# The fourth swish gate tile of each retention head is made among the projections, and the head's work is put in a new order

## The chip, the cores and the metric

The kernel runs on one core of one Trainium2 chip, as one launch. The metric is device time in microseconds (us). TensorE multiplies (PE; its weight load is shown apart as PEld), VectorE (DVE) and ScalarE (ACT) do the arithmetic around it, GpSimd (POOL) does a part of the subtractions and sums, and SyncE (SP) issues most of the loads. All engines run their own instruction stream and meet at semaphores.

## The reference

One layer of a streaming encoder on 640 frames (512 of a new stream, 8 streams of 16 frames): a feed-forward half step, a mixer, a second feed-forward half step, with layer norms between. All matrices are float32. The mixer is what matters here:

```
cb, cc, ch, q, k, v, g, gc, gr = jnp.split(x @ w_in, offsets, axis=-1)
yc, new_buf = short_conv(cc * ch, conv_buf, conv_w)
y_conv = (cb * yc) @ w_conv_br
o, S_new = retention_seq(qh, kh, vh, S0.astype(jnp.float32))      # 4 heads, rotary on q and k
mu = o.mean(-1, keepdims=True)
var = jnp.square(o - mu).mean(-1, keepdims=True)
o = ((o - mu) * lax.rsqrt(var + GN_EPS)).astype(x.dtype).reshape(B, T, D_RET_V)
y_ret = (o * jax.nn.silu(g)) @ w_ret_br
m = jax.nn.sigmoid(gc) * y_conv + jax.nn.sigmoid(gr) * y_ret
return m @ w_out, new_buf, S_new.astype(x.dtype)
```

D_MODEL is 1024, a head has keys of 256 and values of 512, so `g` has 512 columns for each of the 4 heads: four tiles of 128. The states of the 8 running streams (256 x 512 float32 for each head) are read, used and written.

## The kernel before, in words

Each float32 matrix is split into a rounded high part and the low rest, and a product is made as three matmuls (`mm3`, L1034): low by high, high by low, high by high. Activations stand transposed (`xh`, `xl`: 128 partitions x 8 tiles x 640 frames).

Two ways lead to a block of `x @ w`. A unit (L1067) makes one tile of 128 output columns for all 640 frames: 2 halves x 8 tiles of depth x 3 = 48 matmuls of 320 columns. A quad (L1436) makes two such tiles by Winograd's form of Strassen's method: seven products of 4 tiles of depth x 3 = 84 matmuls instead of 96, at the price of sums of weights (POOL, DVE), of their highs (ACT) and lows (DVE), and of sums of the results (DVE). The quads of the mixer are listed in `PROJECTIONS` (L182), 31 of them, in four groups; after each group of four kinds (`cc`, `ch`, `q`, `k`) come swish gates (`s0` to `s5`), merge gates (`gc`, `gr`) and `cb`. `s0` to `s3` hold the first two gate tiles of heads 0 to 3, `s4` and `s5` the third tile of two heads each. A swish quad's result gets its sigmoid from ACT, is multiplied on DVE and is stored to DRAM (`swish_scratch`).

The fourth gate tile of each head was a unit made within the head (`unit_of_chunk`, L1678). Weights for units come in chunks of 512 KB through four slots; PE releases a slot when it is done with the chunk, SP and POOL reload it (raw and high part).

The four heads run one after the other (`head`, L1647). On PE a head is: the values `v` (4 chunks), transposes of rotated keys, scores, `cross(0)` (the queries of half of the running streams by their states; it reads `state`), the outputs of the four prompt tiles (`vh` by `sch`), the gate unit, `cross(1)` (the other half of the streams; all four DMAs of the second state group must have landed), transposes of the normalised outputs (`on`) in four PSUM banks, the first half of the kept state (`knh` by `vh`), the transpose of the sample tile (`on5`), the second half, four state products (`km` by `vp`), and the branch product with `w_ret` (L1624 for its first two units, which wait three times for `head_ready`: for the gated tiles 0 and 1, then 2 and 3, then 4).

On DVE the head takes the statistics of the four prompt tiles, their aggregate, asks ACT for the square root, makes the inverse root with one Newton step and normalises four tiles; it finishes the gate tile; then it does the same chain once more for the sample tile; then five gating products (`ogt`), of each of which ACT makes the high (`ogh`) and DVE the low part (`ogl`), and between them it copies the kept state out of PSUM (`sp`). `psum_free` counts banks that have been read, in order, so a wait for a count is a wait for all reads before it. SP issues the four state loads as soon as `cross(0)` is done (L826), then the load of the gate tiles from `swish_scratch`, then weights.

Of the kernel before, what the change touches and what calls it, by code (L numbers as in the profile page):

```python
# [178 lines left out]
def high_loads_of_slot(c):  # L179
# [3 lines left out]
PROJECTIONS = [(what, j) for j, more in enumerate((("s0", "s1", "gc1"), ("s2", "s3", "gr1"), ("s4", "gc2", "gr2"),  # L183
                                                 ("s5", "gc3")))
# [195 lines left out]
def build_layer(nc, a):  # L380
# [3 lines left out]
    with ctx:  # L384
# [186 lines left out]
        def load_of_part(n):  # L571
# [51 lines left out]
            sem(n) for n in ("swish_sig_made", "swish_made", "swish_in", "k4_made"))  # L623
        conv_ready = sem("conv_ready")
# [61 lines left out]
        U_V, U_K, U_SC, U_O0, U_OP, U_G = 0, 5, 10, 14, 15, 19  # L686
        U_O1, U_T, U_SP, U_T5, U_S1A, U_OUT, U_S1B, U_S0 = 22, 23, 27, 28, 30, 34, 38, 54
# [31 lines left out]
        def _(sync):  # L719
# [102 lines left out]
            def head_loads(i):  # L822
# [7 lines left out]
                sync.dma_start(sg[:, 0:SWISH_TILES, :], a["swish"][i]).then_inc(swish_in, 16)  # L830
# [187 lines left out]
        def _(pe):  # L1018
# [591 lines left out]
            def cross(group, i):  # L1610


                b = bank()
# [7 lines left out]
                last.then_inc(psum_full, 1 + group)  # L1621
                return b
# [24 lines left out]
            def head(i):  # L1647
# [16 lines left out]
                samples = cross(0, i)  # L1664
# [24 lines left out]
                for d in range(2):  # L1689
# [538 lines left out]
        def _(dve):  # L2228
# [689 lines left out]
            def head(i):  # L2918
# [40 lines left out]
                for t in (PT, *range(PT)):  # L2959
                    hi, lo = (knh[:, t, :], knl[:, t, :]) if t < PT else (k4[0][:, :], k4[1][:, :])  # L2960
                    last = split(hi, lo, kd[:, t, :])
                    if t == PT:
                        last.then_inc(k4_made, 1)
                    else:
                        step(last)
# [301 lines left out]
```

## Time and profile before

| | us |
|---|---|
| median of 3 runs | 1758.77 (1758.43 to 1758.84) |
| profiled execution | 1758.78 |
| its span, first to last instruction | 1757.0 |

| engine | busy us | share of the span | instructions |
|---|---|---|---|
| PE | 1746.3 | 99% | 10680 |
| PEld | 1634.4 | 93% | 10680 |
| DVE | 1395.0 | 79% | 1924 |
| ACT | 730.5 | 42% | 1219 |
| POOL | 415.6 | 24% | 296 |

The busy time of a matmul is its time from start to modelled end, and matmuls overlap: in a dense stretch a new one starts every 0.15 us (320 columns) though each is shown as 0.31 us long. So a stretch of matmuls is measured from start to start, not by its mean. Times of DVE and ACT operations can overlap the next one by about 0.1 us in the same way.

### The profile page before, as it was taken

The numbers are of one execution on the slowest core, as the hardware profiler recorded it, in microseconds if no ns is written. First come the engines' busy times: TensorE is split into PE (matmuls) and PEld (weight loads), VectorE is DVE, ScalarE is ACT, GpSimd is POOL, SyncE is SP. The second block draws the span as 40 slices with busy tenths as digits, with TensorE's granted clock in tenths as the row PEclk, the third lists the DMA queues.
The fourth block names the chain that finished last, engine by engine and source line by source line (L and its number), as shares of the span: only waits on it lengthen the run. The fifth ranks groups of instructions, "written<-read, shape, count | busy, mean of one in ns | idle before, by whom it ended". The sixth has DMA issues, their size and how long they took to land.

```text
span 1757.0 us, 27018 instructions
## 1 busy us (share of the span) xinstructions
PE 1746.3 (99%) x10680; PEld 1634.4 (93%) x10680; DVE 1395.0 (79%) x1924; ACT 730.5 (42%) x1219; POOL 415.6 (24%) x296
## 2 busy tenths in 40 slices
PE   9999999999999999999999999999999999999998
PEld 9989999898999999999998989898989989899996
DVE  7888888878898787776267788787868898888986
ACT  5535455443544454544105051414214345454543
POOL 3312112143232223221240212111242212111041
PEclk9999999999999999999999999999999999999999
DMA  8665555434566665733774867676873243333323
GB/s 320 169 185 155 169 156 157 154 98 174 173 184 201 195 193 155 183 95 114 258 241 164 289 216 263 219 257 235 334 288 108 84 129 118 93 105 115 117 93 108
DMA packets 90670, 310.41 MB, mean 177 GB/s; under 512 B 9136, under 2 KB 9520, under 8 KB 90032
## 3 DMA queue, kind: packets, MB, share of 16 engines
q1 hardware_dynamic: 51552, 185.36, 31.2%
q0 software_dynamic: 13696, 50.34, 11.7%
q10 hardware_dynamic: 25296, 72.99, 11.6%
q8 instruction: 85, 1.39, 0.3%
q14 instruction: 41, 0.34, 0.1%
HBM read 267.42 MB, written 75.83 MB: 195 GB/s over the span
## 4 chain that ended last, share of the span: by engine, by line
PE 95%; DVE 3%; issue 1%; ACT 1%; DVEq 0%
PE ps L1024 94%; PE ps L1589 1%; DVE xl L2251 0%; DVE z L2676 0%; DVE z L2779 0%; DVE state L3031 0%; DVE z L2251 0%; PE ps L1498 0%; DVE wql L2251 0%; ACT t L2190 0%; DVE t L2297 0%; ACT xh L1751 0%; DVE y L2814 0%; DVE tl L2251 0%; DVE y L2790 0%
## 5 line engine op out<-in xcount | busy, mean ns | idle before, releaser
L1024 PE MATMUL ps<-th,wql 128*128 128x320 f32 x1136 | 350.9, 309 | 0.0
L1024 PE MATMUL ps<-th,wqh 128*128 128x320 f32 x1136 | 350.7, 309 | 0.0
L1024 PE MATMUL ps<-tl,wqh 128*128 128x320 f32 x1136 | 350.0, 308 | 0.0
L916 POOL TENSOR_TENSOR quad_s<-qraw 128x512 f32<-128x512 f32 x71 | 100.1, 1410 | 709.1 <-DVE wql L2251 322.6
L1024 PE MATMUL ps<-xh,wql 128*128 128x320 f32 x852 | 262.7, 308 | 0.2 <-DVE wql L2251 0.2
L1024 PE MATMUL ps<-xl,wqh 128*128 128x320 f32 x852 | 262.7, 308 | 0.0
L1024 PE MATMUL ps<-xh,wqh 128*128 128x320 f32 x852 | 262.6, 308 | 0.0
L1751 ACT ACTIVATE pu<-ps 128x320 f32<-128x320 f32 x213 | 93.3, 438 | 358.3 <-PE ps L1024 358.3
L2251 DVE TENSOR_TENSOR wql<-quad_s,wqh 128x512 fp32r<-128x512 f32 (+1 forms) x213 | 199.5, 937 | 35.3 <-ACT wqh L1751 34.9
L1024 PEld LDWEIGHTS ps<-tl,wqh 128*128 128x128 f32 x1136 | 213.3, 188 | 0.4
L1024 PEld LDWEIGHTS ps<-th,wql 128*128 128x128 f32 x1136 | 213.2, 188 | 0.4
L1024 PEld LDWEIGHTS ps<-th,wqh 128*128 128x128 f32 x1136 | 213.2, 188 | 0.0
L2251 DVE TENSOR_TENSOR wql<-qraw,wqh 128x512 fp32r<-128x512 f32 x213 | 203.3, 955 | 3.7 <-ACT wqh L1751 3.5
L1751 ACT ACTIVATE wqh<-quad_s 128x512 fp32r<-128x512 f32 (+1 forms) x213 | 163.7, 769 | 53.4 <-PE ps L1024 50.4
L885 POOL TENSOR_TENSOR wl<-raw,wh 128x1024 fp32r<-128x1024 f32 x52 | 131.3, 2526 | 127.4 <-DMA wh<-in_weights 42.2
L1024 PEld LDWEIGHTS ps<-xh,wql 128*128 128x128 f32 x852 | 159.9, 188 | 1.0 <-DVE wql L2251 0.4
L1024 PEld LDWEIGHTS ps<-xl,wqh 128*128 128x128 f32 x852 | 160.0, 188 | 0.4
L1024 PEld LDWEIGHTS ps<-xh,wqh 128*128 128x128 f32 x852 | 160.0, 188 | 0.0
L1751 ACT ACTIVATE wh<-raw 128x1024 fp32r<-128x1024 f32 x67 | 70.3, 1050 | 173.4 <-DMA raw<-in_weights 122.5
L1751 ACT ACTIVATE wqh<-qraw 128x512 fp32r<-128x512 f32 x213 | 132.8, 624 | 10.4 <-PE ps L1024 10.4
L922 POOL TENSOR_TENSOR quad_s<-qraw 128x512 f32<-128x512 f32 x71 | 110.4, 1554 | 67.8 <-DVE wql L2251 67.8
L2251 DVE TENSOR_TENSOR quad_s<-quad_s,qraw 128x512 f32<-128x512 f32 x138 | 105.9, 767 | 23.2 <-POOL quad_s L916 15.6
(293 smaller groups left out, 3764.1 us busy)
## 6 DMA issues: line engine op xcount, KB each, us to landing
qraw<-in_quads SPq DMA_DIRECT2D x142, 512.0 KB, 3.7
raw<-in_weights SPq DMA_DIRECT2D x92, 512.0 KB, 4.6
wh<-in_weights POOLq DMA_DIRECT2D x57, 512.0 KB, 5.2
raw<-sums_scratch SPq DMA_DIRECT2D x32, 512.0 KB, 3.9
state<-in_state_ret ACTq DMA_DIRECT2D x32, 512.0 KB, 7.4
out_ret_sample<-state ACTq DMA_DIRECT2D x32, 512.0 KB, 5.0
sums_scratch<-in_sum_add POOLq DMA_DIRECT2D x8, 1024.0 KB, 9.3
sums_scratch<-sums_scratch POOLq DMA_DIRECT2D x16, 512.0 KB, 6.2
```

Source lines behind the costliest of these rows:

```text
L885: pool.tensor_tensor(w_lo(r), w_raw(r), w_hi(r).bitcast(f32), ALU.subtract).then_inc(chunk_split, 1)
L916: pool.tensor_tensor(qs[:, 0, :], qraw[:, c0, 512:1024], qraw[:, c1, 512:1024], ALU.add).then_inc(pool_sums, 1)
L922: pool.tensor_tensor(qs[:, 2, :], qraw[:, c0, 0:512], qraw[:, c0, 512:1024], ALU.add).then_inc(pool_sums, 1)
L1024: ins = nc.tensor.matmul(out, lhs, rhs, start=start, stop=stop, skip_group_check=adds)
L1589: last = nc.tensor.transpose(cols(k, 128, ps[:, b, :]), src, ident[:, :])
L1751: return nc.scalar.activation(out, in_, ACT.Copy, **kw)
L2251: return V.tensor_tensor(out, x, y, op)
```

## The change

Two quads, `s6` and `s7`, are added to the projections (33 instead of 31); they make the fourth gate tile of two heads each. The gate units, their chunks and what ACT and DVE did for them in the heads are gone. Within a head PE now does `cross(1)` right after the four prompt outputs, then both halves of the kept state, then all transposes, then the state products. DVE takes the sample tile's statistics with the others and runs one chain for five tiles. The copies of the kept state move to ACT.

```diff
-HEAD_CHUNKS = 9
-SWISH_TILES = 3
+HEAD_CHUNKS = 8
-HEAD_BANKS = 62
+HEAD_BANKS = 60
-PROJECTIONS = [... ("s4", "gc2", "gr2"), ("s5", "gc3") ...]
+PROJECTIONS = [... ("s4", "s6", "gc2", "gr2"), ("s5", "s7", "gc3") ...]
-    return [(n, 0), (n, 1)] if n < H else [(2 * (n - H) + m, 2) for m in range(2)]
+    return [(n, 0), (n, 1)] if n < H else [(2 * (n % 2) + m, 2 + (n - H) // 2) for m in range(2)]
...
-                sync.dma_start(sg[:, 0:SWISH_TILES, :], a["swish"][i]).then_inc(swish_in, 16)
+                sync.dma_start(sg[:, :, :], a["swish"][i]).then_inc(swish_in, 16)
...
# PE, head
-                samples = cross(0, i)
+                samples = bank()
+                cross(0, i, samples).then_inc(psum_full, 1)
...
-                assert bk.at - u0 == U_G
-                unit_of_chunk()
-                bk.add()
-                assert bk.at - u0 == U_O1
-                assert cross(1, i) == samples
-                pe.wait_ge(psum_free, u0 + U_G)
-                for dp in range(2):
-                    for t in range(0, PT, 2):
-                        transposed([cols(2 * dp + k, 128, on[:, t + n, :]) for n in range(2) for k in range(2)])
                 assert bk.at - u0 == U_SP
+                assert (u0 + U_O1) % 8 == samples
+                cross(1, i, samples).then_inc(cross_made, 1)
+                pe.wait_ge(keys_split, i + 1)
                 for d in range(2):
...
-                    last.then_inc(psum_full, 1)
-                    if d == 0:
-                        assert bk.at - u0 == U_T5
-                        pe.wait_ge(psum_free, u0 + U_T + 1)
-                        transposed([cols(k, 128, on5[:, :]) for k in range(4)])
+                    last.then_inc(psum_full, 1 + 2 * d)
+                bk.add(2)
+                assert bk.at - u0 == U_T
+                pe.wait_ge(psum_free, u0 + U_SP)
+                for dp in range(2):
+                    for t in range(0, PT, 2):
+                        transposed([cols(2 * dp + k, 128, on[:, t + n, :]) for n in range(2) for k in range(2)])
+                assert bk.at - u0 == U_T5
+                pe.wait_ge(psum_free, u0 + U_T)
+                pe.wait_ge(sp_kept, 2 * i + 2)
+                transposed([cols(k, 128, on5[:, :]) for k in range(4)])
                 assert bk.at - u0 == U_S1A
                 state_products(1, (0, 1))
...
# ACT, head
-                roots(0, PT)
-                gate(0)
-                gate(1)
-                roots(5, 6)
+                roots(0, PT + 1)
+                def kept_product(d):
                     b = full()
+                    copy(sp[:, d, :], ps[:, b, :]).then_inc(sp_kept, 1)
+                kept_product(0)
+                act.wait_ge(packed, i * 24 + 24)
+                masked_keys(1)
+                kept_product(1)
+                for n in range(5):
+                    gated_hi(n)
...
# DVE, head
-                    if c == PT - 1:
-                        branch_low(i, 0)
+                    if c >= PT - 2:
+                        branch_low(i, c - (PT - 2))
                     banks.append(full())
                     step(V.bn_stats(stats[:, c, 0:6], ps[:, banks[c], :]))
+                dve.wait_ge(cross_made, i + 1)
+                step(V.bn_stats(stats[:, PT, 0:6], ps[:, samples, :]))
...
-                inv_root(0, PT, GN_EPS)
+                inv_root(0, PT + 1, GN_EPS)
                 for c in range(PT):
-                    normalise(banks[c], c, on[:, c, :])
+                    normalise(banks[c], c, on[:, c, :], 1 if c < PT - 1 else 3)
+                normalise(samples, PT, on5[:, :], 2)
                 dve.wait_ge(swish_in, 16 * (i + 1))
...
                 gated(0)
-                inv_of_root(5, 6)
-                normalise(b5, 5, on5[:, :], 2)
                 gated(1)
-                dve.wait_ge(psum_free, bk(-1))
                 gated_lo(0)
-                after()
-                gated(2)
-                dve.wait_ge(psum_free, bk(-1))
                 gated_lo(1)
                 signal_head()
+                gated(2)
                 gated(3)
                 gated_lo(2)
-                if i:
-                    dve.wait_ge(sp_out, i * 16)
-                kept_product(0)
                 after()
                 gated(4)
                 gated_lo(3)
                 signal_head()
-                kept_product(1)
                 gated_lo(4)
                 signal_head()
```

The first place is PE in a head, from the last output product of the prompt tiles to the transposes of the normalised outputs. `vh,sch` is the last output product, `xh,wl` begins the gate unit, `state,qx` is a cross product, `ident,on` a transpose, `vh,knl` begins a half of the kept state. Before (the 46 rows of the unit between the second and the third are left out):

```order
L1024 MATMUL ps<-vh,sch 128x512
L1024 MATMUL ps<-xh,wl 128x320 [waits psum_free,chunk_split]
...
L1024 MATMUL ps<-xh,wh 128x320
L1024 MATMUL ps<-state,qx 32x512 [waits state_in2,state_in1,state_in3,state_in0,psum_free]
L1024 MATMUL ps<-state,qx 32x512 x7
L1589 MATMUL ps<-ident,on 128x128 [waits psum_free]
```

and in the changed kernel (of the kept state's 24 rows those that wait are shown):

```order
L1024 MATMUL ps<-vh,sch 128x512
L1024 MATMUL ps<-state,qx 32x512 [waits state_in2,state_in3,state_in1,state_in0]
L1024 MATMUL ps<-state,qx 32x512 x7
L1024 MATMUL ps<-vh,knl 128x512 [waits psum_free,keys_split]
...
L1024 MATMUL ps<-vh,knl 128x512 [waits psum_free]
...
L1589 MATMUL ps<-ident,on 128x128 [waits psum_free]
```

The cross product that waits for the states moved ahead by the 48 matmuls of the unit, and the kept state now stands between it and the transposes, no longer behind them.

The second place is DVE in a head, from the normalising of the prompt tiles (`on`) to the last signal to PE before the branch product (each MEMSET of `rt` that waits for dve_step, behind an `ogl`, is such a signal). Before, the piece up to the first signal, without the chain's four small rows:

```order
L2888 TENSOR_SCALAR on<-ps,mv,rt 128x512 x3
L2251 TENSOR_TENSOR sg<-ps,sg 128x320 [waits psum_full,act_done]
L2251 TENSOR_TENSOR wl<-raw,wh 128x1024 [waits hi_loaded2,raw_loaded2]
...
L2991 BN_STATS stats<-ps 128x6 [waits psum_full,swish_in]
...
L2251 TENSOR_TENSOR ogt<-ps,sg 128x512 [waits psum_full]
...
L2888 TENSOR_SCALAR on_97<-ps,mv,rt 128x512 [waits dve_step]
...
L2251 TENSOR_TENSOR ogl<-ogt,ogh 128x2x2x128 [waits act_done,psum_free]
L2251 TENSOR_TENSOR ogt<-ps,sg 128x512 [waits psum_full,dve_step]
```

and in the changed kernel:

```order
L2968 BN_STATS stats<-ps 128x6 [waits cross_made]
...
L2878 TENSOR_SCALAR on<-ps,mv,rt 128x512 x3
L2878 TENSOR_SCALAR on_97<-ps,mv,rt 128x512
L2241 TENSOR_TENSOR ogt<-ps,sg 128x512 [waits psum_full,swish_in]
L2241 TENSOR_TENSOR ogt<-ps,sg 128x512 [waits psum_full]
L2241 TENSOR_TENSOR ogl<-ogt,ogh 128x2x2x128 [waits act_done] x2
L2883 MEMSET rt 128x1 [waits dve_step]
L2241 TENSOR_TENSOR ogt<-ps,sg 128x512 [waits psum_full] x2
```

The statistics of the sample tile, which wait for the cross product, stand ahead of the four normalisations instead of behind them.

## Rows read from the trace of the kernel before

**Rows 1.** The page's busy times, and the chain that ended last.
```profile
PE 1746.3 (99%) x10680; PEld 1634.4 (93%) x10680; DVE 1395.0 (79%) x1924; ACT 730.5 (42%) x1219; POOL 415.6 (24%) x296
PE 95%; DVE 3%; issue 1%; ACT 1%; DVEq 0%
```

**Rows 2.** Waits of PE: total us, times, longest. The longest of four.
```profile
PE ps L1024 <- DVE ones L2869: 1.3, 1, 1.3
```

**Rows 3.** Timeline of PE in the second head: start, us, operation, count.
```profile
1040.77 0.31 PE L1024 MATMUL ps<-xh,wl 128*128 128x320 f32 x1
...
1047.90 1.92 PE L1024 MATMUL ps<-state,qx 128*32 128x512 f32 x16
1049.75 1.97 PE L1589 MATMUL ps<-ident,on 128*128 128x128 f32 x16
1051.47 0.48 PE L1024 MATMUL ps<-vh,knl 128*128 128x512 f32 x1
...
1054.67 0.48 PE L1024 MATMUL ps<-vh,knl 128*128 128x512 f32 x1
...
1057.52 1.07 PE L1024 MATMUL ps<-vp,km 128*128 128x512 f32 x4
1058.43 0.31 PE L1024 MATMUL ps<-ogh,wl 128*128 128x320 f32 x1
```

**Rows 4.** Busy times in a stretch of the projections: PE, PEld, DVE, ACT, POOL, clock.
```profile
480.00:840.00 360.00, 360.00 (x2460) 360.00 (x2460) 281.40 (x377) 168.06 (x295) 96.43 (x72) 1.00 0.57 164
```

**Rows 5.** State loads for the second cross product; landings of heads 1, 2, 3, 4.
```profile
L826 SPq DMA_DIRECT2D state<-in_state_ret x1: 469/469/469, 1034.7 to 1034.7; - x1
DMA to landing us min/median/max: 3.9/5.2/6.5
DMA to landing us min/median/max: 3.8/5.8/7.6
DMA to landing us min/median/max: 3.8/5.2/6.4
DMA to landing us min/median/max: 4.7/6.1/7.4
```

**Rows 6.** Timeline of DVE in the second head.
```profile
1041.71 0.18 DVE L2976 BATCH_NORM_AGGREGATE mv<-stats 128x2 f32<-128x6 f32 x1
...
1043.58 2.97 DVE L2888 TENSOR_SCALAR on<-ps,mv,rt 128x512 f32<-128x512 f32 x4
...
1049.96 0.70 DVE L2991 BATCH_NORM_STATS2 stats<-ps 128x6 f32<-128x512 f32 x1 [0.99 <-PE ps L1024]
1050.70 0.18 DVE L2994 BATCH_NORM_AGGREGATE mv<-stats 128x2 f32<-128x6 f32 x1
...
1052.61 0.81 DVE L2888 TENSOR_SCALAR on<-ps,mv,rt 128x512 f32<-128x512 f32 x1
...
1058.05 0.68 DVE L2251 TENSOR_TENSOR ogt<-ps,sg 128x512 f32<-128x512 f32 x1
1058.64 0.68 DVE L2251 TENSOR_TENSOR ogl<-ogt,ogh 128x512 fp32r<-128x512 f32 x1
...
1059.39 0.06 DVE L2893 MEMSET rt<- 128x1 f32 x1
...
1060.72 0.06 DVE L2893 MEMSET rt<- 128x1 f32 x1
```

**Rows 7.** Timeline of ACT in the second head: high parts of gated tiles.
```profile
1051.70 0.63 ACT L1751 ACTIVATE ogh<-ogt 128x512 fp32r<-128x512 f32 x1 [0.40 <-DVE ogt L2251]
...
1056.19 1.15 ACT L1751 ACTIVATE ogh<-ogt 128x512 fp32r<-128x512 f32 x2
```

**Rows 8.** PE's first matmuls of the program, and the last stretch's busy times.
```profile
1.26 4.63 PE L1024 MATMUL ps<-ones 128*128 128x320 f32 x16 [1.26 <-DVE ones L2869]
...
1747.00:1757.00 10.00, 1.85 (x9) 1.19 (x7) 7.18 (x14) 1.54 (x3) 0.00 (x0) 0.85 0.65 205
```

More of the change, by code:

```diff
@@ L181, in high_loads_of_slot @@
     return sum(SLOTS[e] == SLOTS[c] and high_by_cast(e) for e in range(FIRST_HI, c + 1))
-PROJECTIONS = [(what, j) for j, more in enumerate((("s0", "s1", "gc1"), ("s2", "s3", "gr1"), ("s4", "gc2", "gr2"),
-                                                 ("s5", "gc3")))
+PROJECTIONS = [(what, j) for j, more in enumerate((("s0", "s1", "gc1"), ("s2", "s3", "gr1"), ("s4", "s6", "gc2", "gr2"),
+                                                 ("s5", "s7", "gc3")))
                for what in ("cc", "ch", "q", "k") + more + ("cb",)]
@@ L623, in build_layer @@
             sem(n) for n in ("swish_sig_made", "swish_made", "swish_in", "k4_made"))
+        keys_split, cross_made, sp_kept = sem("keys_split"), sem("cross_made"), sem("sp_kept")
         conv_ready = sem("conv_ready")
@@ L1608, in state_products, with cross @@
                     last.then_inc(psum_full, 2)
-            def cross(group, i):
-                b = bank()
+            def cross(group, i, b):
                 for bb in range(4):
@@ L1620, in cross @@
                                   (group, d) == (0, 0), True, adds=(group, d) != (0, 0))
-                last.then_inc(psum_full, 1 + group)
-                return b
+                return last
             def first_branch_units(w_ofs):
@@ L2110, in head @@
                 pack(kp, 2, k4[1])
-                roots(0, PT)
-                bk.add(U_G - U_SC)
-                def gate(half):
+                roots(0, PT + 1)
+                bk.add(U_SP - U_SC)
+                def kept_product(d):
                     b = full()
-                    result(nc.scalar.activation(cols(half, HALF, sg[:, SWISH_TILES, :]), ps[:, b, 0:HALF], ACT.Sigmoid))
-                act.wait_ge(packed, i * 24 + 12)
-                gate(0)
-                gate(1)
+                    copy(sp[:, d, :], ps[:, b, :]).then_inc(sp_kept, 1)
[3 more added lines that the diff above has]
+                kept_product(1)
+                bk.add(2)
                 def gated_hi(n):
@@ L2963, in head @@
                         last.then_inc(k4_made, 1)
+                    elif t == PT - 1:
+                        last.then_inc(keys_split, 1)
                     else:
@@ L2973, in head @@
                 after()
                 V.memset(rt[:, 3, 0:1], 0.0)
-                for c in range(PT):
+                for c in range(PT + 1):
                     step(V.bn_aggr(mv[:, c, :], stats[:, c, 0:6]))
                 after()
-                inv_root(0, PT, GN_EPS)
+                inv_root(0, PT + 1, GN_EPS)
                 for c in range(PT):
-                    normalise(banks[c], c, on[:, c, :])
-                for half in range(2):
-                    act_result()
-                    s, b = cols(half, HALF, sg[:, SWISH_TILES, :]), full()
-                    tt(s, ps[:, b, 0:HALF], s, ALU.mult).then_inc(psum_free, 1)
-                    if half == 0:
-                        branch_low(i, 1)
@@ L2997, in head @@
+                normalise(samples, PT, on5[:, :], 2)
+                dve.wait_ge(swish_in, 16 * (i + 1))
                 gated(0)
-                inv_of_root(5, 6)
-                normalise(b5, 5, on5[:, :], 2)
                 gated(1)
-                dve.wait_ge(psum_free, bk(-1))
                 gated_lo(0)
-                after()
-                gated(2)
-                dve.wait_ge(psum_free, bk(-1))
                 gated_lo(1)
                 signal_head()
+                gated(2)
@@ L3255 @@
     args["z_scratch"] = nc.dram_tensor("z_scratch", (128, TT, D), mybir.dt.float32, kind="Internal").ap()
-    for name, shape in (("qk", (H, 2, 128, 2, NT)), ("swish", (H, 128, SWISH_TILES, NT)), ("gate_c", (128, KT, NT)), ("gate_r", (128, KT, NT)),
+    for name, shape in (("qk", (H, 2, 128, 2, NT)), ("swish", (H, 128, 4, NT)), ("gate_c", (128, KT, NT)), ("gate_r", (128, KT, NT)),
                         ("mix", (128, KT, NT)),
```

29 lines of the change are left out of this document (5 added, 24 removed).

## The prediction

> **What bounds the kernel now.** I read the page's busy times first: PE is busy for 99% of the span, and the chain that ended last is PE for 95% [rows 1]. The waits of PE come next: four kinds, the longest in total 1.3 us, and that one at the very start [rows 2]. So PE is never kept waiting in the middle of the program, and a change is worth what it takes from PE's own instructions, less every wait that it opens. The timeline of PE in one head [rows 3] then gives what each piece takes from start to start, and those of DVE and ACT beside it [rows 6, 7] what they need between two of PE's pieces.
>
> **PE's own instructions.** Per matmul of 320 columns the projections show 360 us / 2460 = 0.1463 us [rows 4]. Two more quads are 2 x 84 = 168 matmuls: +24.6 us. In the head the gate unit takes, from its first matmul to the cross product, 1047.90 - 1040.77 = 7.13 us [rows 3]; four of them: -28.5 us. Everything else on PE is the same work in another order. The difference is -3.9 us, and that is all that the change can gain.
>
> I cost nothing to the new quads on the other engines. DVE is busy 281 of 360 us in the projections and ACT 168 [rows 4], and two swish quads next to each other are in that stretch already (s0 and s1, s2 and s3) without a wait of PE. If that cover failed, one late sum would cost PE some tenths of a us in 2 quads. What DVE and ACT are spared in the heads (the gate tile's two sigmoids with their table loads, its two products, two copies, one norm chain) is worth nothing, as it is not what PE waits for.
>
> **What was hidden behind the gate unit.** The unit stood between the last prompt output and the second cross product. In those 7.13 us the last state load landed, DVE ran the norm chain and normalised four tiles. And the kept state's 5.7 us stood behind the transposes, as cover for the gating. Now the kept state must cover the norm chain, and nothing is left to cover the gating but the fifth transpose and the four state products. I lay the head out anew, with the end of the last prompt output as zero (1040.77 in the second head).
>
> 1. State loads. The last of four is issued at 1034.7 and lands 7.6 us later, at 1042.3 [rows 5]: 1.5 us after zero. Its issue hangs on the first cross product, so it lies as far ahead of zero in every head, and the landings of 6.5, 6.4 and 7.4 us in the others give 0.4, 0.3 and 1.3. PE waits there in each head, with all its later work queued behind: 1.5 + 0.4 + 0.3 + 1.3 = 3.6 us in all (3.5 to 3.7 by rounding). The kernel before reached this product 7.13 us later and never saw it. Both ends of this term: nothing, if the landing is a little faster than shown, and about 1.5 us in every head, 6.2 us. I take the 3.6. The larger gate load behind the states is issued after them and I let it cost nothing.
>
> From here, times count from the start of the cross product.
>
> 2. Norm chain. Cross product to statistics: 1049.96 - 1047.90 = 2.06. Statistics to aggregate: 0.74. First aggregate to first normalisation: 1043.58 - 1041.71 = 1.87, and 0.10 for a fifth aggregate. Four normalisations: 2.97 [rows 3, 6]. Sum: 7.74; the transposes can start at 7.79. PE gets there at 1.85 (cross) + 5.70 (kept state: 24 matmuls, twice 1057.52 - 1054.67 = 2.85) = 7.55 [rows 3]. Wait: 0.24.
>
> 3. First gated tiles. One normalisation follows the next after (2.97 - 0.81) / 3 = 0.72, so the sample tile is normalised and DVE goes on to gating at 7.65 + 0.72 = 8.37. A gating product follows the next after 0.59 and lasts 0.68; ACT starts its high part 0.04 after that end and needs 0.63, the second 0.6 later [rows 6, 7]. So: products at 8.37 and 8.97, highs done at 9.72 and 10.29, lows at 9.76 and 10.36, and 0.75 after the start of a low the signal (1058.64 to 1059.39): 11.11, at PE 11.2. PE: transposes 1.72 to 9.51, the fifth 0.35 (3.20 - 2.85) to 9.86, state products 0.91 to 10.77. Wait: 0.43.
>
> 4. First six branch matmuls, 0.88: 12.08. The next six need the fourth gating product read (the counter of freed banks), which DVE begins after the signal: 11.13, 11.73, done 12.41. Wait: 0.4, then 0.88: 13.33.
>
> 5. Second signal: low 2 at 12.5, product 4 at 13.2 (it waits for that low), then 1058.05 to 1059.39 = 1.34 as shown: 14.55, at PE 14.6. Wait: 1.27. Twelve matmuls, 1.76: 16.36. The third signal is at about 15.4, ahead of PE, as it was before (1060.72 against 1058.43 + 24 x 0.147 = 1061.96). From there on both kernels do the same with the same lead.
>
> So the waits are 0.24 + 0.43 + 0.40 + 1.27 = 2.3 us in each head, 9.4 us in four, besides the states. Checked as a whole: the second half of the first two branch units began 21.18 us after zero before; it now begins at 16.36 and the wait for the states. Four heads: 4 x (16.36 - 21.18) + 3.6 = -15.7 us. With the quads, +24.6: **+8.9 us**. The profiled execution took 1758.78 (span 1757.0, 1.8 around it), the median of the runs is 1758.77; the forecast is 1767.7 us, 0.5% slower.
>
> The copies of the kept state on ACT I cost at nothing: ACT has only the root and the masked keys between the packing and the first gated tile, and a copy of 128x512 from PSUM ends in about what a high part takes, 0.6 us [rows 7]; the second is done some 1 us before the fifth transpose needs its bank. If it is late, that 0.35 us piece waits, but the gating chain beside it decides anyway.
>
> **A rule on the clock.** The granted clock is 1.00 in the projections [rows 4]. In the last 10 us, where PE is busy for 1.85, it is 0.85, and the first 16 matmuls of the program are 0.29 us apart, twice the 0.147 of later ones [rows 8]: those are the levels of 1.2 and 2.4 GHz. The waits above are 1.5 us at most, with dense work between. The Trainium skill, TensorE: Matmul & The Clock Gate, section HAM oscillation — how this bites in real kernels, says that waits between bursts of matmuls can send the array back to half rate each time; by that rule the heads would pay more than their waits. The trace has no wait in mid-program to test it on; as a rival it has its price below.
>
> **Rivals.**
> (a) The gating and norm waits stand, the states don't make PE wait: 1767.7 - 3.6 = 1764.1. For it: the landings of two heads miss by only 0.4 us. Against: two miss by 1.3 and more. 13%.
> (b) Faster than before: the waits of a head stay under 0.97 us (3.9 / 4), because DVE's chain is not as serial as I sum it. With none the time is 1754.9. For it speaks that the kept state all but covers the norm chain (7.55 against 7.79). Against: the second signal alone needs five normalisations, five products and four lows after the cross product, 14.5 us, where PE has 12.7 us of work. Faster 5%; another 6% that it ends within 0.2% of before.
> (c) The clock drops in each head: about 4.6 us at half rate as in the opening [rows 8], so 2.3 us lost, 9.2 in four heads: 1776.9. Against: waits are short and broken up. 4%.
> (d) PE falls behind in the projections as well, since DVE gets two more quads' worth of splits and swish products. At worst a wait as long as one swish product and its sigmoid, under 3 us in all: 1770. 5%.
> The forecast itself, with its own range of 1765 to 1771: 67%.
>
> **Range and chances.** The range takes in (a) and the upper end of the states (+2.6): 1762.5 to 1772. What 3 runs of this kernel can tell apart is about 0.2%, 3.5 us. Faster by more than that 0.05, within it 0.07, slower 0.88.
>
> **What would show it.** In the waits of PE: in each head a wait for the state DMA of 0.3 to 1.5 us ahead of the cross product; one for DVE's normalised tiles of about 0.2 ahead of the transposes; and three for the gating in the branch product, together about 2 us, the longest 1.3. The second half of the first branch units starts 16.4 us after the cross product. The projections grow by 24.6 us with no wait. If PE shows no waits in the heads, the layout above is wrong and the time is near 1755; if PE's clock falls there, (c) is right.

## The result, and the profile after

The changed kernel takes 1770.17 us (median of 6 runs, 1768.84 to 1774.42) against 1758.67 (6 runs, 1758.42 to 1759.04): a ratio of 1.0068, with an interval of 1.0057 to 1.0078. The forecast was 1767.7 with a range of 1762.5 to 1772. The profiled execution of the changed kernel is its fastest run, 1768.84 us, with a span of 1766.8 against 1757.0: 9.8 us more.

First the page's busy times of the changed kernel, with the chain that ended last:

```profile
PE 1747.4 (99%) x10656; PEld 1630.7 (92%) x10656; DVE 1396.2 (79%) x1902; ACT 734.2 (42%) x1229; POOL 411.1 (23%) x292
PE 91%; DVE 5%; DMA 1%; ACT 1%; issue 1%; SPq 0%; DVEq 0%
```

PE still shows 99% and has 24 matmuls fewer than in [rows 1]; a busy share of 99% doesn't tell 1757 from 1767. The chain does: PE's part fell from 95% to 91%, and a DMA is in it now. Next the waits of PE in the changed kernel (total us, times, longest):

```profile
PE ps L1024 <- DVE rt L2883: 4.4, 4, 1.1
PE ps L1024 <- DMA state<-in_state_ret: 2.1, 4, 1.1
PE ps L1024 <- issue: 1.4, 4, 0.3
PE ps L1024 <- DVE ones L2859: 1.3, 1, 1.3
PE ps L1024 <- DVE xl L2241: 0.6, 2, 0.4
PE ps L1024 <- DVE z L2241: 0.3, 1, 0.3
...
```

The first three lines come four times each, once a head, and none of them is in [rows 2]: the second signal of the gating, the state loads, and the first signal ("issue" is a wait that the view can't put down to an engine; in the second head PE goes on at 1073.23, 0.16 us after the signal's MEMSET at 1073.07). The wait of 0.2 us for DVE's normalised tiles that the forecast had ahead of the transposes is too short for this view: the kept state's last matmul starts at 1069.07 and PE could have gone on at about 1069.30, but the transposes start at 1069.56. The state loads before the cross product, in heads 1, 3 and 4, in the timeline of PE:

```profile
974.54 1.92 PE L1024 MATMUL ps<-state,qx 128*32 128x512 f32 x16 [0.42 <-DMA state<-in_state_ret]
...
1150.08 1.92 PE L1024 MATMUL ps<-state,qx 128*32 128x512 f32 x16 [1.14 <-DMA state<-in_state_ret]
...
1237.41 1.92 PE L1024 MATMUL ps<-state,qx 128*32 128x512 f32 x16 [0.29 <-DMA state<-in_state_ret]
```

From the end of the last prompt output (the forecast's zero) to the start of this cross product the four heads lose 0.58, 0.37, 1.30 and 0.45 us, 2.7 in all. The second head, which answers to [rows 3], on PE:

```profile
1061.87 1.92 PE L1024 MATMUL ps<-state,qx 128*32 128x512 f32 x16 [0.21 <-DMA state<-in_state_ret]
...
1069.56 2.40 PE L1589 MATMUL ps<-ident,on 128*128 128x128 f32 x20
1071.71 1.17 PE L1024 MATMUL ps<-vp,km 128*128 128x512 f32 x4
...
1073.23 0.39 PE L1024 MATMUL ps<-ogh,wl 128*128 128x320 f32 x1 [0.34 <-issue]
...
1076.63 0.42 PE L1024 MATMUL ps<-ogh,wl 128*128 128x320 f32 x1 [1.09 <-DVE rt L2883]
```

and on DVE, which answers to [rows 6]:

```profile
1063.85 0.70 DVE L2968 BATCH_NORM_STATS2 stats<-ps 128x6 f32<-128x512 f32 x1 [1.46 <-PE ps L1024]
1064.59 0.18 DVE L2972 BATCH_NORM_AGGREGATE mv<-stats 128x2 f32<-128x6 f32 x1
...
1066.54 3.68 DVE L2878 TENSOR_SCALAR on<-ps,mv,rt 128x512 f32<-128x512 f32 x5
...
1073.07 0.06 DVE L2883 MEMSET rt<- 128x1 f32 x1
...
1076.51 0.06 DVE L2883 MEMSET rt<- 128x1 f32 x1
...
1077.30 0.06 DVE L2883 MEMSET rt<- 128x1 f32 x1
```

Behind the states, what PE waits for is DVE's each time: DVE works from 1063.85 to 1076.5 with no gap above 0.1 us but the root's 0.27, and the three MEMSETs are the three signals. Before, the prompt tiles' aggregates began 6.19 us ahead of the cross product (1041.71 against 1047.90); now they begin 2.72 us behind its start (1064.59 against 1061.87).

Where the 9.8 us come from: what stands ahead of the heads is longer by 24.6 (the end of the first head's prompt outputs moved from 949.34 to 973.95). From there to the second half of the first branch units took 21.18 us before; now it takes 16.64 and the state wait, in each head alike within 0.01. That is 4 x (21.18 - 16.64) = 18.2 less, and 2.7 more for the states: 24.6 - 18.2 + 2.7 = 9.1. The other 0.7 is lost in the last head's end, of which the forecast said nothing:

```profile
1279.60 1.55 PE L1024 MATMUL ps<-vp,km 128*128 128x512 f32 x6
1281.49 0.71 PE L1024 MATMUL ps<-vp,km 128*128 128x512 f32 x2 [0.34 <-DVE z L2241]
```

The eight last state products take 2.55 us there and 1.89 before. The trace leads from this wait back to the stores of the states. ACT issues the third set of state loads only when the second set's stores have landed, and its four high parts `xh` stand behind these loads in its queue; DVE waits for them, and PE for DVE:

```profile
1276.09 2.14 ACTq L2005 DMA_DIRECT2D state<-in_state_ret  x4
1278.28 2.62 ACT L1747 ACTIVATE xh<-z 128x640 fp32r<-128x640 f32 x4 [17.88 <-issue]
```

```profile
1279.05 1.56 DVE L2241 TENSOR_TENSOR xl<-z,xh 128x640 fp32r<-128x640 f32 x2 [1.87 <-ACT xh L1747]
```

The four stores, issued from 1254.3 to 1261.3, landed 9.6 to 14.7 us after issue. In the kernel before they took 8.3 to 12.8 us, but there PE reached its last state products 3.15 us behind the start of ACT's high parts (1270.51 against 1267.36) and not 1.3 (1279.60 against 1278.28).

That the median lies another 1.3 us above the profiled run, and that six runs are 5.6 us apart where the kernel before has 0.6, the forecast did not have either; the experiments come back to it. The 0.6 is that of six runs on one chip: beside the experiments the kernel before itself lay between 1757.9 and 1762.4 (11 runs) on one chip and between 1757.9 and 1765.8 (21 runs) on another.

### The profile page after: what moved, and what is told of

It is laid out like the page before. It is cut to its first block, busy times and chain, and to the rows that moved or that the text cites. A ratio compares the mean times of both kernels' runs of the same rounds, so it can differ in the third digit from the quotient of the medians.

```text
span 1766.8 us, 26953 instructions
## 1 busy us (share of the span) xinstructions
PE 1747.4 (99%) x10656; PEld 1630.7 (92%) x10656; DVE 1396.2 (79%) x1902; ACT 734.2 (42%) x1229; POOL 411.1 (23%) x292
## 3 DMA queue, kind: packets, MB, share of 16 engines
q10 hardware_dynamic: 25296, 72.99, 11.5%
## 4 chain that ended last, share of the span: by engine, by line
PE 91%; DVE 5%; DMA 1%; ACT 1%; issue 1%; SPq 0%; DVEq 0%
PE ps L1024 90%; DMA state<-in_state_ret 1%; DVE on L2878 1%; DVE ogl L2241 1%; DVE ogt L2241 0%; DVE xl L2241 0%; PE ps L1589 0%; DVE z L2241 0%; DVE z L2666 0%; DVE z L2769 0%; SPq L826 0%; ACT ogh L1747 0%; DVE state L3000 0%; PE ps L1498 0%; DVE wql L2241 0%
## 5 line engine op out<-in xcount | busy, mean ns | idle before, releaser
L1024 PE MATMUL ps<-th,wql 128*128 128x320 f32 x1168 | 360.7, 309 | 0.0
L1024 PE MATMUL ps<-th,wqh 128*128 128x320 f32 x1168 | 360.6, 309 | 0.0
L1024 PE MATMUL ps<-tl,wqh 128*128 128x320 f32 x1168 | 359.9, 308 | 0.0
L916 POOL TENSOR_TENSOR quad_s<-qraw 128x512 f32<-128x512 f32 x73 | 102.8, 1409 | 730.3 <-DVE wql L2241 362.8
L1024 PE MATMUL ps<-xh,wql 128*128 128x320 f32 x876 | 270.0, 308 | 0.2 <-DVE wql L2241 0.2
L1024 PE MATMUL ps<-xl,wqh 128*128 128x320 f32 x876 | 270.1, 308 | 0.0
L1024 PE MATMUL ps<-xh,wqh 128*128 128x320 f32 x876 | 270.0, 308 | 0.0
L1024 PEld LDWEIGHTS ps<-th,wqh 128*128 128x128 f32 x1168 | 219.3, 188 | 0.0
L2241 DVE TENSOR_TENSOR wql<-qraw,wqh 128x512 fp32r<-128x512 f32 x219 | 212.0, 968 | 3.7 <-ACT wqh L1747 3.5
L885 POOL TENSOR_TENSOR wl<-raw,wh 128x1024 fp32r<-128x1024 f32 x48 | 122.8, 2560 | 126.8 <-DMA wh<-in_weights 44.9
L922 POOL TENSOR_TENSOR quad_s<-qraw 128x512 f32<-128x512 f32 x73 | 113.8, 1558 | 71.9 <-DVE wql L2241 71.9
```

Source lines behind the costliest of these rows:

```text
L885: pool.tensor_tensor(w_lo(r), w_raw(r), w_hi(r).bitcast(f32), ALU.subtract).then_inc(chunk_split, 1)
L916: pool.tensor_tensor(qs[:, 0, :], qraw[:, c0, 512:1024], qraw[:, c1, 512:1024], ALU.add).then_inc(pool_sums, 1)
L922: pool.tensor_tensor(qs[:, 2, :], qraw[:, c0, 0:512], qraw[:, c0, 512:1024], ALU.add).then_inc(pool_sums, 1)
L1024: ins = nc.tensor.matmul(out, lhs, rhs, start=start, stop=stop, skip_group_check=adds)
L2241: return V.tensor_tensor(out, x, y, op)
```

## The experiments

Theory: PE is the limit, the change saves it 3.9 us, and it opens waits in each head because the gate unit covered the state loads and DVE's serial norm and gating. Rivals: the quads cost more than their instructions; the waits come from where the chain and the state loads stand in the order, and a better order gives them back. The numbers in front of a result are the median and the range of its runs, with the ratio to the kernel before on the same chip (1759.13 us there for the first four, 1758.4 to 1758.8 for the rest). The changed kernel was not run again beside them, so a difference of medians to it is one between chips, and its own runs lie 5.6 us apart; the traces are the firmer ground.

**The quads alone** (the kernel before, with the two swish quads made and saved and not read):

```diff
-... ("s4", "gc2", "gr2"), ("s5", "gc3") ...
+... ("s4", "s6", "gc2", "gr2"), ("s5", "s7", "gc3") ...
```

> The kernel before with the two extra swish quads among the projections (made, gated and stored, but not read by the heads; heads as before). Theory (the quads cost their 168 matmuls and nothing else): +24.6 us, 1783.4, PE without a wait in the projections. Rival (DVE falls behind there): 1785 to 1787, with waits of PE for DVE in the projections.

1784.29 us (1783.2 to 1787.76), ratio 1.0144 [1.0131, 1.0157]; span 1781.7, which is 24.7 over the kernel before, for 24.6 forecast. The view lists no wait of PE between 430 and 970 us, where the projections lie. So this half of the sum is shown by itself, and what the change gives back lies in the heads alone. The runs do not all agree: two of the four, without a trace, are at 1785.1 and 1787.8, in the rival's range or above it. But the kernel before has single runs 2 to 3 us above its median on this chip too.

**No wait for the second group's states** (the changed kernel; the second cross product reads the first group's states and leaves out the second group's, which is loaded behind it):

```diff
-                    pe.wait_ge(state_in[bb], i * 48 + 16 * (group + 1))
+                    pe.wait_ge(state_in[bb], i * 48 + 16)
```

> The changed kernel, but the second cross product reads the states of the first group (its numbers are left wrong), and the second group is loaded behind it, so that PE has no DMA to wait for there. Theory: 2.7 us less than the profiled 1768.8, so about 1766, and the runs, which spread over 5.6 us for the changed kernel, lie within 1 us of each other, because it is the landing of the states that differs from run to run. Rival (the spread and the 2 us above the profiled run come from elsewhere): same median gap of 2 to 4 us but the spread stays; or no gain, if DVE's chain absorbs the wait.

1770.96 us (1767.31 to 1772.34), 1.0061 [1.0049, 1.0073]. The waits at the cross product are gone and the heads follow each other after 86.97 to 87.00 us (they took 87.54, 87.29 and 88.17). The gating's waits stay as they were, to the tenth. But the time didn't fall by the 2.7 us, since another wait has come up in the last head, on DVE's side behind the third set of state loads, the last of which landed 10.9 us after issue (6.9 in the changed kernel's trace):

```profile
1286.33 1.40 DVE L3000 SCALAR_TENSOR_TENSOR state<-state,ht,ps 128x512 f32<-128x512 f32 x2 [3.38 <-DMA state<-in_state_ret]
```

```profile
PE ps L1024 <- DVE state L3000: 3.1, 1, 3.1
```

```profile
1287.22 0.47 PE L1024 MATMUL ps<-wh,xl 128*128 128x512 f32 x1 [3.08 <-DVE state L3000]
```

So I missed with the spread: the runs still lie 5.0 us apart, and the wait at the cross product is not what sets them apart.

**The order of the gating on DVE** (the changed kernel):

```diff
                 gated_lo(2)
-                after()
-                gated(4)
                 gated_lo(3)
                 signal_head()
+                gated(4)
                 gated_lo(4)
```

> The changed kernel with DVE's low part of gated tile 3 ahead of the gating product of tile 4, so that the second signal to PE comes about 0.7 us earlier; the third comes a little late then. Theory (PE waits for DVE's serial gating): 0.5 us less in each head, 2.0 us in all, and the wait of 1.1 us for the second signal becomes about 0.4. Rival (that wait is set by the state DMA or by ACT's high parts): no change.

1769.56 us (1768.38 to 1773.95), 1.0059 [1.0047, 1.0071]. The second signal's wait fell from 1.1 to 0.4 us a head, and 0.25 of it came back at the third signal:

```profile
PE ps L1024 <- DMA state<-in_state_ret: 2.5, 4, 0.9
PE ps L1024 <- DVE state L2999: 1.7, 1, 1.7
PE ps L1024 <- DVE rt L2883: 1.5, 4, 0.4
```

A head less its loss at the cross product takes 86.73 us instead of 86.92: 0.2 where I expected 0.5. The medians (0.6 us apart) can't show that; the trace does. The second line is the wait of the run before, here 1.7 us and without that run's edit: it comes and goes with the landing of the third set.

**The norm chain under the kept state** (the changed kernel; the kept state's first half ahead of the cross product, so that only 2.85 us cover the chain):

```diff
-                cross(1, i, samples).then_inc(cross_made, 1)
                 pe.wait_ge(keys_split, i + 1)
                 for d in range(2):
+                    if d == 1:
+                        cross(1, i, samples).then_inc(cross_made, 1)
```

> The changed kernel with the first half of the kept state (2.85 us) ahead of the second cross product. The states have landed by then. Theory (the norm chain starts only with the cross product's end, and everything behind hangs on it): the transposes start 2.85 + 7.69 us after the last prompt output instead of 0.67 + 7.69, so +2.2 us in each head, +8.7 in all, 1777.6. Rival (what counts is PE's work and the state wait): 2.7 us faster than the changed kernel.

1778.6 us (1777.17 to 1779.51), 1.0107 [1.0094, 1.012]: slower by 8.4 than the changed kernel, 8.7 over it expected. (The profiled spans are 10.9 us apart, with one wait of 1.87 us in the projections, which the edit doesn't touch.) PE's waits, and its granted clock (the column behind POOL) around the transposes of the first head:

```profile
PE ps L1589 <- DVE on L2879: 11.2, 4, 2.8
```

```profile
980.00:985.00 5.00, 3.70 (x20) 2.17 (x12) 3.70 (x16) 2.77 (x7) 0.00 (x0) 1.00 0.28 107
985.00:990.00 5.00, 3.50 (x17) 3.51 (x18) 4.26 (x8) 1.26 (x2) 0.00 (x0) 0.58 0.00 0
990.00:995.00 5.00, 5.00 (x26) 4.61 (x25) 4.69 (x11) 1.86 (x3) 0.00 (x0) 0.74 0.00 0
```

```profile
986.50 4.53 PE L1589 MATMUL ps<-ident,on 128*128 128x128 f32 x20 [2.80 <-DVE on L2879]
```

Two things are shown. The five-tile chain does hang on the cross product, and 2.85 us of cover less give 2.80 us of wait in each head; the states' wait is gone, as they have longer to land. And behind a wait of 2.8 us, with short transposes after it, the clock falls in three of the four heads: the 20 transposes take 4.53, 3.56 and 4.07 us instead of 2.40. This is my rival (c), which the changed kernel itself does not show: its waits in the heads are 1.1 us at most, and every 5 us of its heads have a clock of 1.00. The Trainium skill, TensorE: Matmul & The Clock Gate, section HAM oscillation — how this bites in real kernels, warns of such bursts with waits between; three heads of this run agree, and the changed kernel's shorter waits don't bring it on. In the fourth head the same wait left the clock at 1.00, and so did the wait of 3.08 us in the run without the state wait, which had matmuls of 512 columns behind it. So the length of the wait alone doesn't decide, and what does isn't shown. The slower transposes cost PE little here: the state products behind the first branch units start 23.64, 22.99, 23.59 and 22.98 us after the last prompt output, the last of these at full clock, so 0.7, 0 and 0.6 us, because DVE's gating is the later one anyway.

**The last head's transfers.** gate_r and mix, 5.2 MB, are read in the last head, beside its state loads and stores. Here they are issued earlier, from 4.1 us ahead of the head's last prompt output instead of 8.6 us behind it:

```diff
-            sync.wait_ge(psum_full, HEADS_BANKS + (H - 1) * HEAD_BANKS + U_T)
             for n in range(KT // 2):
...
-                if n in (0, 2):
-                    load(1)
...
-            load(KT)
+            load(KT + 2)
```

The last head's last two weight loads, which stood among them, come behind them here.

> The changed kernel with the loads of gate_r and mix (2 x 2.6 MB) in the last head issued right behind that head's load of the swish tiles, some 10 us earlier than now, instead of behind the kept state; all work is the same. Theory: they are what makes the last head's state loads and stores land late, and so both the 0.7 us that this head takes more than the others in the profiled run and most of the 5 us by which single runs differ. Then the profiled run takes 0.7 us less than the changed kernel's (about 1768.1), the median falls by 1.5 to 2 us to about 1768.4, and the runs lie within 2 us of one another. Rival: the spread comes from transfers elsewhere (the state loads ahead of the cross product in all four heads): then at most 0.7 us goes, the median is 1769.5 or more, and the runs still differ by 4 us or more.

1768.13 us (1767.4 to 1769.55), 1.005 [1.0037, 1.0063]: the median is 2.0 us lower, and the spread 2.2 us instead of 5.6. Both are what the theory had, but five runs here and six there, on different chips and with intervals of the ratios that overlap, don't show either. The trace shows the last head's end: the second set's stores land 3.9 to 6.7 us after issue instead of 9.6 to 14.7, ACT's high parts are early, and the eight last state products take 1.90 us. The profiled run is the slowest of the five, as it drew 3.7 us of state waits.

**Three repairs together**: the kept state's first half, then cross product, transposes, second half; the sample tile with a chain of its own; the low halves and the loads as in the two runs before.

```diff
+                kept_state(0).then_inc(psum_full, 4)
+                cross(1, i, samples).then_inc(cross_made, 1)
...
+                        transposed([cols(2 * dp + k, 128, on[:, t + n, :]) ...
+                kept_state(1).then_inc(kept_made, 1)
```

> The changed kernel with the gate_r and mix loads early (as in the run beside it) and three things in each head: TensorE makes the first half of the kept state, then the second group's cross product, the transposes, and only then the second half; the sample tile has a norm chain of its own again; gated_lo(3) stands ahead of gated(4). Theory (the waits of the changed kernel come from one chain that hangs on the cross product, and from VectorE's order behind it): the wait for the state loads (0.6 us a head), the 0.3 us ahead of the first transposes and 0.7 of the 1.1 us at the second signal go, but VectorE has the second chain's small operations more, which keep it the later one at the second signal: zero to second signal about 14.0 us in place of 15.4; total 1768.8 - 4 x 1.1 - 0.7 = 1763.7 in the profiled run, between 1761 and 1766. No drop of the granted clock, since no wait ahead of the transposes passes 1.1 us. Rival: VectorE's whole work between the last prompt output and the third signal (about 14 us) is what counts, however it is ordered: then it stays within 1 us of the run beside it (about 1767.5 to 1768.5).

1763.33 us (1762.79 to 1764.12), 1.0021 [1.0012, 1.003]: 6.8 us of the 11.5 are back, where 1763.7 was expected. The waits of PE that stand in the heads now:

```profile
PE ps L1587 <- DVE on L2886: 4.4, 4, 1.1
...
PE ps L1022 <- ACT sp L1752: 1.0, 4, 0.3
```

Neither the states nor the second signal is among them. The larger one hangs on DVE, and four normalisations stand in it; the smaller is for ACT's copy of the kept state. Which of the edits gave how much isn't separated.

**DVE's work given to ACT**: two prompt tiles and the sample tile are normalised by ScalarE.

```diff
+                    return nc.scalar.activation(out, ps[:, b, :], ACT.Identity, bias=rt[:, 3, c:c + 1],
+                                                scale=rt[:, 2, c:c + 1])
```

> As the run before it, with two of the four prompt tiles and the sample tile normalised by ScalarE (Identity with scale and bias), which takes 3 x 0.74 us off VectorE in each head and puts as many on ScalarE beside it, plus two small operations. If VectorE's work is what TensorE waits for behind the kept state, each head becomes up to 1.4 us shorter than with the order alone: about 1758 in the profiled run (between 1755 and 1761), at or a little under the kernel before, whose floor by TensorE's own work is 1754.9. If ScalarE is late in its turn (its normalising, 4 masked keys and 2 copies of the kept state stand ahead of the first high half), or if the activation tables are exchanged for it, there are new waits of 1 us or more a head for ScalarE, and it stays at 1763 or above.

1761.22 us (1760.62 to 1762.57), 1.0013 [1.0004, 1.0022]. The 1.1 us ahead of the transposes are gone, in each head, but a head is only 0.7 us shorter (85.79 for 86.47) and not 1.4, and the profiled run, at 1762.55, misses its 1755 to 1761. It has 1.10 us once in the last head, where DVE waits 1.05 us for a weight load that stands behind the early gate_r and mix loads: my own edit to the loads. And in every head DVE waits 0.77 us for a high half that stands behind the sample's normalising on ACT:

```profile
1069.26 1.29 DVE L2261 TENSOR_TENSOR ogl<-ogt,ogh 128x512 fp32r<-128x512 f32 x2 [0.77 <-ACT ogh L1753]
```

**ACT's order** (the last version; the first high half first, two masked keys later, the kept state's second half in another bank, the two last weight loads ahead of gate_r and mix), and **the same with gate_r and mix later again**:

```diff
+                    if n == 1:
+                        sample()
...
+            load(2)
             for n in range(KT // 2):
```

> The last version (three tiles normalised by ScalarE) with ScalarE's queue in another order: the first high half ahead of the sample's normalising, and the masked keys of slots 2 and 3 behind the second copy of the kept state; that second product in another bank, so that the first state product needn't wait for its copy; and in the last head the two weight loads ahead of the gate_r and mix loads. By the trace of the last version, VectorE waits 0.77 us in each head for the first high half, which the sample's normalising (0.78 us) stands ahead of; behind it TensorE loses 0.26 and 0.24 us at the second and third signal and 0.25 us for the kept state's copy, and about 0.1 us more at each of the three restarts; and 1.1 us once in the last head, behind a weight load that lands late. Theory: these go, 0.9 us a head and 1.1 us once: 1760.5 - 3.6 - 1.1 = 1755.8 us of span in the profiled run, median 1756.8 (between 1755.5 and 1758.5), under the kernel before by 0.1%. Rival: VectorE's order was no limit, TensorE's losses there are of another kind (restarts behind any wait on a semaphore): then only the 1.1 us goes and the median is about 1760.

> As the run beside it, but the gate_r and mix loads of the last head go out only once the first half of the kept state is made, as late as in the changed kernel. If these loads collide with the last head's state traffic, its tail is 0.7 us or more later than in the run beside it and the runs lie 4 us apart instead of 1.5; if the load of the last weights was all that mattered, the two are within 0.3 us.

1760.37 us (1759.04 to 1761.49), 1.0008 [1.0, 1.0017], and 1760.01 us (1759.45 to 1760.38), 1.0008 [0.9999, 1.0017]. I had expected 1756.8 for the first. The 1.1 us in the last head are gone, and most of DVE's wait, but of PE's loss in a head only 0.3 us went with it (from the end of the prompt outputs to the state products behind the first branch units 18.59 us for 18.87). What stays is 0.45 us at the copy of the kept state's second half and 0.6 at the second and third signal. In the second run the first branch didn't come: the later gate_r and mix loads cost nothing, and the runs lie within 0.9 us. But they were not as late as in the changed kernel, as I had written. They wait for the kept state's first half, which ends earlier in this order: they go out from 2.9 us behind the last prompt output, where the changed kernel has 8.6 and the first of the two runs is 3.2 us ahead of it. So this pair shows neither that lateness costs nothing nor that the order of the weight loads is what counts.

**Another bank for the kept state, and DVE's and ACT's order once more**:

```diff
+                bk.add(-8)
+                kept_state(1).then_inc(kept_made, 1)
+                bk.add(8)
...
+                state_products(1, (0, 1), 0)
...
                 gated_lo(0)
+                after()
+                gated(2)
                 gated_lo(1)
```

> The last version (e10, gate_r and mix loads late) with the losses taken away that its trace still shows in each head, 1.05 us between the last prompt output and the state products behind the first branch units: (1) 0.45 us where the second state product waits for the copy of the kept state's second half out of its bank: that half now lies in a bank that none of these products needs, and the sample tile's transposes come behind them; (2) 0.6 us at the second and third signal, of which VectorE's waits for ScalarE's high halves make up about half (0.17, 0.42 us): gated(2) goes between the two first low halves, and the masked keys of slots 2 and 3 behind the last high half. Theory: TensorE's own work is the limit then but for 0.3 us a head: a head of 84.7 instead of 85.54 us, the profiled run 1757.7 - 3.3 = 1754.4 us of span, the median 1756.7 (1755.5 to 1758), 0.1% under the kernel before. Rival: the losses move on to the third signal, whose high and low half of the sample tile (1.4 us from one engine to the other) nothing hides: then half of the gain, median 1758.4, no difference from before.

1758.39 us (1757.51 to 1758.77) against 1758.44, ratio 0.9999 [0.999, 1.0008]: the rival was right, the loss at the third signal stays. PE has no wait in the heads that the view lists, and the page's first lines are

```profile
span 1755.7 us, 26988 instructions
...
PE 1745.0 (99%) x10656; PEld 1630.1 (93%) x10656; DVE 1384.7 (79%) x1926; ACT 743.1 (42%) x1245; POOL 408.6 (23%) x292
```

A head takes 85.07 us. The kernel before takes 91.42, of which the gate unit is 7.13, so 84.3 would be PE alone: 0.8 us a head are still lost, 3.1 in all, and that is nearly the whole 3.9 us that there was to gain. In the stretch from the first branch matmul to the next state products, 7.66 us against 7.04 before, are 0.6 of them:

```profile
1069.38 0.60 PE L1589 MATMUL ps<-ident,on 128*128 128x128 f32 x4
...
1077.40 1.09 PE L1024 MATMUL ps<-vp,km 128*128 128x512 f32 x4
```

```profile
1071.50 0.69 DVE L2272 TENSOR_TENSOR ogt<-ps,sg 128x512 f32<-128x512 f32 x1
...
1072.89 0.69 DVE L2272 TENSOR_TENSOR ogl<-ogt,ogh 128x512 fp32r<-128x512 f32 x1 [0.70 <-ACT ogh L1758]
1073.65 0.06 DVE L2914 MEMSET rt<- 128x1 f32 x1
```

The sample tile's product, its high half on ACT and its low half on DVE run one behind the other, and the third signal at 1073.65 is what PE waits for. No version beats the kernel before by what can be measured.

## Why the prediction was right

The sign, the size and the mechanism held. By its own steps:

- PE's own instructions, +24.6 and -28.5: right. The first is measured alone (+24.7 of span), and the projections of the changed kernel are longer by 24.6 without a wait.
- Step 1, state loads: 2.7 us measured in the profiled run for 3.6 forecast. The landings were 6.5, 6.3, 7.2 and 6.4 us after issue in heads 1 to 4, where I had taken 6.5, 7.6, 6.4 and 7.4 from before. The loss is the landing less 5.9 us in every head, so the mechanism held and the landings didn't. A landing time belongs to a run, not to a head: another run of nearly the same kernel lost 3.7. The bounds, 0 to 6.2, were the honest statement; that the single value came within 1 us was luck.
- Step 2, norm chain: the transposes started 7.69 us after the cross product for 7.79. The run with 2.85 us less cover lost 2.80.
- Steps 3 and 4, first signal and the fourth gating product: the branch began at 11.36 for 11.2, and its second six matmuls at 12.52 for about 12.45.
- Step 5, second signal: 14.76 us for 14.6, alike in all four heads within 0.02. The second half began at 16.64 for 16.36: 0.28 us a head, 1.1 in all. Some 0.1 of it is DVE's, whose MEMSETs came at 11.20 and 14.64 for 11.11 and 14.55. The rest are PE's restarts: it went on 0.16 and 0.12 us behind these MEMSETs, where I had allowed 0.09 and 0.05, and the second matmul behind the wait started 0.25 us after the first instead of 0.15.
- The sum: +8.9 for 9.8 in the profiled spans. -0.9 from the states, +1.1 from signals and restarts, and +0.7 from the end of the last head, which is the one term that I had not written down at all. There ACT's queue stands until the second set's stores have landed, while with no gate unit PE comes to the head's end sooner.
- One number beside the sum is wrong: under (b) I gave PE 12.7 us of work up to the second signal. The pieces of steps 2 to 5 are 7.55 + 1.72 + 0.35 + 0.91 + 1.76 = 12.3. No term hangs on it.
- The rivals: (a) is out, the states do make PE wait in all four heads. (b) is out: the change is slower, and a series of further edits brings the time back to that of the kernel before (1758.39 against 1758.44) and not below it. (c) is out for this kernel at a clock of 1.00; at a wait of 2.8 us the clock did fall in three heads. (d) is out for the profiled run. Three experiments show one wait in the projections each, of 0.66, 1.87 and 0.29 us, all at 504 to 506 us, which is ahead of the first swish quad of any (its product is stored at 525): these are not the new quads' doing.
- The median is 2.5 us over the forecast, and the profiled run 1.1. The difference between these two is the runs' spread, which I had given no term; that the median still lies in the range owes something to its width.

What stays open: which of the last head's transfers makes the second set's stores land late. They took 9.6 to 14.7 us in the changed kernel and 3.8 to 7.6 in every run with gate_r and mix issued earlier, whether or not the weight loads went first; the two edits weren't tried one by one on the changed kernel. The spread has no single source in the traces. The same code ahead of the heads ends its first prompt outputs between 973.8 and 976.0 us in the profiled runs, the state waits come to 2.1, 2.5 and 3.7 us, and the wait behind the third set to 0, 1.7 and 3.1.

## What to carry to other kernels

Before taking out work of the engine that is the bound, ask what lay under it: here 7.1 us of matmuls covered a landing, a norm chain of another engine and, through the piece behind them, the gating. What is won is the instructions less every wait that comes up, and the waits behind another engine can be laid out beforehand from the starts of one head, here to 0.3 us. A cover that the same engine must run anyway is worth its length only as long as the chain under it is shorter; if it is taken away, the chain must be cut in the same edit (tiles of their own, work on a third engine, other banks), and all of that together gained nothing here.

Give a term to the end of a stage and to the spread between runs: where transfers of several kinds meet, a profile of one run is one draw.

## What the runs showed of the hardware

The clock: a wait of 2.8 us with 20 transposes of 128 columns behind it brought the granted clock down to 0.58 over 5 us in one head, and to 0.79 and 0.67 in two others, but left it at 1.00 in the fourth; a wait of 3.08 us with matmuls of 512 columns behind it left it at 1.00; waits of 1.1 us in four heads, with a second one of 0.3 us some 3 us earlier, left it at 1.00. The last of the four 512 KB state loads of the second group landed between 6.3 and 7.6 us after issue in the traces before and after; the last of the third group, in the last head, after 6.9 us in the changed kernel and 10.9 in the run without the state wait. Stores of the states, 512 KB each, behind 5.2 MB of other loads took up to 14.7 us in the changed kernel and up to 12.8 in the kernel before, and 6.7 at most with those loads issued 12.7 us earlier. PE went on 0.12 to 0.16 us after the MEMSET on DVE that released it. ScalarE normalised a tile of 128x512 from PSUM in 0.78 us, near DVE's 0.81, with no load of its tables within the heads beside square roots and copies.
